# RWKV bonus sums: per-pair columns of ones as weights, tokens streamed in two column tiles

## The reference, cut to what matters

```python
r_h, k_h, v_h, a_h = heads(r), heads(k), heads(v), heads(a)
y = wkv7_scan(r_h, decay, k_h, v_h, -kk, kk * a_h)
mean = jnp.mean(y, -1, keepdims=True)
var = jnp.mean(jnp.square(y - mean), -1, keepdims=True)
y = ((y - mean) * lax.rsqrt(var + GN_EPS)).reshape(B, S, D)
y = y * ln_w.astype(f32) + ln_b.astype(f32)
bonus = jnp.sum(r_h * k_h * r_k.astype(f32), -1, keepdims=True) * v_h
y = (y + bonus.reshape(B, S, D)).astype(h.dtype)
return (y * g) @ w_o
```

## Time and profile before

| | |
|---|---|
| median of 3 runs | 1690.89 us (1688.22 to 1691.16) |
| profiled execution | 1693.16 us, span 1691.3 us |
| PE busy | 1655.3 us (98%) |
| DVE, ACT, POOL busy | 64%, 56%, 67% |
| mean granted clock of TensorE | 0.996 of full speed |

### The profile page before, as it was taken

How to read it: one execution, slowest core, us unless ns; L and a number is a source line. 1 busy time by engine, 2 the same in 40 slices (tenths; PEclk the granted TensorE clock), 3 DMA queues, 4 the chain that set the end, 5 groups by cost and what they waited for, 6 DMA issues and landing times.

```text
span 1691.3 us, 32104 instructions
## 1 busy us (share of the span) xinstructions
PE 1655.3 (98%) x11894; PEld 1459.8 (86%) x11894; DVE 1075.0 (64%) x1978; ACT 948.4 (56%) x1417; POOL 1134.6 (67%) x504
## 2 busy tenths in 40 slices
PE   8999999999999999999999999999999999999998
PEld 6888889999999998887787878888888899888887
DVE  5324242997546666678898985455557975755555
ACT  5458553445544444555555657666567842356555
POOL 6974776788889898786676447665577451746463
PEclk9999999999999999999999999999999999999999
DMA  8544444566655555689999945465553412155552
GB/s 306 200 149 144 155 150 175 163 197 188 189 169 172 155 161 156 195 311 349 357 380 403 411 180 178 182 204 194 191 169 113 168 27 78 53 189 187 196 185 76
DMA packets 96095, 330.10 MB, mean 195 GB/s; under 512 B 32928, under 2 KB 33456, under 8 KB 78592
## 3 DMA queue, kind: packets, MB, share of 16 engines
q1 hardware_dynamic: 84544, 295.06, 51.4%
q0 software_dynamic: 11312, 33.68, 5.3%
q10 hardware_dynamic: 144, 0.07, 0.0%
HBM read 322.47 MB, written 5.24 MB: 194 GB/s over the span
## 4 chain that ended last, share of the span: by engine, by line
PE 59%; POOL 14%; issue 8%; DVE 8%; ACT 7%; DMA 3%; DVEq 0%; ACTq 0%; POOLq 0%; SPq 0%
POOL rows_lo L3115 7%; PE bank L897 7%; PE bank L903 4%; PE bank L1092 4%; PE bank L640 4%; PE bank L1236 4%; PE bank L646 4%; PE bank L641 4%; POOL stat L3146 3%; PE bank L1113 3%; PE bank L929 3%; DMA gathered<-in_v,picked_row 3%; PE bank L972 2%; ACT up_hi L1995 2%; PE bank L1096 2%
## 5 line engine op out<-in xcount | busy, mean ns | idle before, releaser
L3100 POOL TENSOR_TENSOR unit_lo<-unit_raw,unit_hi 128x2048 fp32r<-128x2048 f32 (+1 forms) x86 | 337.3, 3943 | 147.1 <-ACT unit_hi L1715 120.9
L3115 POOL TENSOR_TENSOR rows_lo<-rows_raw,rows_hi 128x1024 fp32r<-128x1024 f32 x128 | 309.4, 2418 | 72.9 <-ACT rows_hi L1835 46.0
L3190 POOL TENSOR_TENSOR up_lo<-up_raw,up_hi 128x2048 fp32r<-128x2048 f32 x22 | 111.2, 5056 | 156.6 <-ACT up_hi L1995 126.8
L1913 ACT ACTIVATE rows_hi<-rows_raw 128x1024 fp32r<-128x1024 f32 x128 | 135.8, 1061 | 124.3 <-PE bank L972 101.4
L2678 DVE TENSOR_TENSOR rows_lo<-rows_raw,rows_hi 128x1024 fp32r<-128x1024 f32 x128 | 159.2, 1249 | 25.3 <-ACT rows_hi L1913 22.0
L1715 ACT ACTIVATE unit_hi<-unit_raw 128x2048 fp32r<-128x2048 f32 x70 | 134.0, 1919 | 65.4 <-PE bank L646 36.8
L1092 PE MATMUL bank<-x_lo_hi,up_hi 128*128 128x512 f32 x640 | 159.8, 392 | 0.0
L903 PE MATMUL bank<-x_lo_hi,rows_lo 128*128 128x256 f32 x1024 | 143.3, 283 | 0.5 <-POOL rows_lo L3115 0.5
L903 PEld LDWEIGHTS bank<-x_lo_hi,rows_lo 128*128 128x128 f32 x1024 | 135.7, 190 | 6.4 <-POOL rows_lo L3115 0.9
L3153 POOL DMA_INDIRECT gathered<-in_v,picked_row x64 | 92.4, 1444 | 69.9 <-DVE bank L2668 57.8
L1092 PEld LDWEIGHTS bank<-x_lo_hi,up_hi 128*128 128x128 f32 x640 | 116.2, 189 | 21.6
(11 more groups left out here) (509 smaller groups left out, 4185.2 us busy)
## 6 DMA issues: line engine op xcount, KB each, us to landing
unit_raw<-in_ring SPq DMA_DIRECT2D x69, 1024.0 KB, 4.9
rows_raw<-in_u SPq DMA_DIRECT2D x128, 512.0 KB
rows_raw<-in_v SPq DMA_DIRECT2D x128, 512.0 KB
up_raw<-in_up SPq DMA_DIRECT2D x44, 1024.0 KB, 5.0
down_raw<-in_down SPq DMA_DIRECT2D x22, 1024.0 KB, 4.9
unit_raw<-in_ring SPq DMA_DIRECT2D x20, 256.0 KB, 3.7
kept_hidden<-table SPq DMA_DIRECT2D x16, 256.0 KB, 4.1
const<-in_const SPq DMA_DIRECT2D x1, 1792.0 KB, 14.2
```

The costliest lines, as they stand in the source:

```text
L1913: A(rows_hi[q % 2][:, :], rows_raw[q][:, :], ACT.Copy).then_inc(S("v_hi_ready"), 1)
L3100: return nc.gpsimd.tensor_tensor(unit_lo[SLOT_OF[n]][:, w], unit_raw[SLOT_OF[n]][:, w], hi, ALU.subtract)
L3115: nc.gpsimd.tensor_tensor(rows_lo[q][:, :], rows_raw[q][:, :], rows_hi_f[q % 2], ALU.subtract).then_inc(S("u_lo_ready"), 1)
```

## The change

The weights become 16 columns of ones and zeros. `two_heads` is a strip of 32 columns with two columns of ones in its middle (one for each half of the partitions), and `pair_of_heads(p)` is a window of 16 columns on it whose ones stand in columns 2p and 2p + 1. The tokens stream: for each pair, 128 columns of `bonusT` for each half of the tokens, into partitions 0 to 15 (th = 0) and 64 to 79 (th = 1) of one bank, `("bh",)`, where the eight pairs add up. ScalarE copies the two 16x128 results to `by_head_bonus`. TensorE goes on with `x_of_chunk(3)` and then turns them to tokens with one product each (16 rows, identity of 16 columns) into the same `("bo", th)` as before, which ScalarE copies on as before. GpSimd fills the strip with three memsets while it sets up the mixer, ahead of the signal `zeroed`.

```diff
+    two_heads = view("two_heads", CONST_AT["iota"][0] + DK, [4 * PAIRS])
+    pair_of_heads = lambda p: two_heads[:, 2 * (PAIRS - p):2 * (PAIRS - p) + 2 * PAIRS]
+    by_head_bonus = view("by_head_bonus", EXTRA_AT + 512, [P])
+    of_heads = lambda th: slice(DK * th, DK * th + 2 * PAIRS)
...
-            def bonus_sums(th):
-                o = fill(("bo", th))
+            def bonus_by_head():
+                o = fill(("bh",), TC)
+                ends = [None] * TC
                 for p in range(PAIRS):
-                    t = mm(o[:, 2 * p:2 * p + 2], bonusT[:, p, th * P:(th + 1) * P], C("head_ones")[:, 0:P:DK], start=True, stop=True)
-                full(("bo", th), t)
+                    for th in range(TC):
+                        ends[th] = mm(o[of_heads(th), 0:P], pair_of_heads(p), bonusT[:, p, th * P:(th + 1) * P], start=p == 0, stop=p == PAIRS - 1, skip_group_check=True)
+                full_by_heads(("bh",), ends)
+
+            def bonus_turned():
+                wait_drained(pe, ("bh",))
+                for th in range(TC):
+                    r = of_heads(th)
+                    o = fill(("bo", th))
+                    full(("bo", th), mm(o[:, 0:2 * PAIRS], by_head_bonus[r, :], ident[r, r], start=True, stop=True))
...
+            pe.wait_ge(S("zeroed"), 1)
             pe.wait_ge(S("bonus_scaled"), 1)
-            for th in range(TC):
-                bonus_sums(th)
+            bonus_by_head()
             c = NRC - 1
             x_of_chunk(c)
+            bonus_turned()
             pe.wait_ge(S("vst_loaded"), 16 * 8)
             step_rhs(0)
...
+            def bonus_by_head():
+                o = wait_filled(act, ("bh",))
+                for th in range(TC):
+                    t = A(by_head_bonus[of_heads(th), :], o[of_heads(th), 0:P], ACT.Copy)
+                drain(("bh",), t)
+
...
+            bonus_by_head()
             for th in range(TC):
                 bonus_sums(th)
...
+            step(nc.gpsimd.memset(two_heads[:, :], 0.0))
+            for par in range(2):
+                step(nc.gpsimd.memset(two_heads[head(par), 2 * PAIRS + par:2 * PAIRS + par + 1], 1.0))
             step(nc.gpsimd.memset(starts[:, :], 1.0))
```

## The result

The median after is 1699.89 us (1695.66 to 1702.18, 6 runs) against 1690.22 us for the kernel before in as many runs beside it: 1.0058 times as long, 95% interval 1.0045 to 1.0071. The profiled execution has a span of 1700.0 us, 8.7 more.

What follows compares the result with a forecast made beforehand. TensorE (PE), busy 98% of the span, was taken as the bound. Wait 10.81 + products 12.59 - 12.75 before = 10.65 us later, less 4.1 gained: 6.55 us slower, 1697.4 us; range 1693.6 to 1702.0, first case's own 1694.5 to 1701.

Steps and rivals of the forecast that it cites:

- the gain: Bonus stretch: 9.61 us become 5.00, 4.61 less; about 0.5 us lost waiting at r2, 4.1 us left.
- the products behind the wait: Output products of the first tokens: 10.89 us plus 1.7 us for a low clock after idling, 12.59 us.
- the wait: First output products: fill on bank 0 waits for the drain of chunk 3's output, 10.81 us later.
- the forecast's first case: Gain of 4.1 us at the bonus, output products wait on bank 0: 1697.4 us, chance 0.71.
- its marks: Fast new sums, full clock through 1425, PE idle about 11 us before the output products, then half clock there.
- rival 2: Bonus stretch: low clock not the old sums' doing, or comes with new ones; gain 2.3 us, 1699.2 us, chance 0.12.
- Rival 4: New bonus sums: the two column tiles don't overlap, 1.87 us more, +8.4 us, 1699.3 us, chance 0.04.
- The shifts: GpSimd's two `rows_shift` behind the bonus delay `first_sum(3)`, so chunk 3's `r2` waits about 0.5 us.
- I let it all move by 4.1 us: Recurrence and chain behind chunk 3's `r2`: all of it moves earlier by the 4.1 us left of the bonus gain.
- the bound of 2.3: Lower bound of the gain left from the bonus stretch, 2.3 us, taken from the low-clock case.
- Rival 5: Output products don't wait, since chunk 3's output is drained in time; only the gain is left, 1686.8 us, chance 0.06.
- Rival 3: Output products: the wait comes, but the clock holds or is back at once; +4.9 us, 1695.7 us, chance 0.07.

Runs made afterwards that it cites:

- the loads spread: Changed kernel with chunk 3's output fixed in bank 7, plus pieces of the first three output-weight units issued after later fills: median 1688.86 us, ratio 0.9982.
- the turn only: Kernel before, with the turn of the banks moved one further ahead of the bonus sums and nothing else: 1700.5 us against 1690.1, ratio 1.0057.
- bank 7: Changed kernel with chunk 3's output put into bank 7 by a fixed number, not the bank of chunk 2's output: 1688.48 us against 1690.1, ratio 0.9991.

## Why the prediction came true, and which terms were off

The forecast was +6.55 us, 1697.4 as a median, own range 1694.5 to 1701; the ratio stands for 9.8 us (7.6 to 12.0), the profile for 8.88. So 1699.89 is inside the range, but 6.55 us is less than the interval allows: three terms were off, the gain by 1.8 us and the products behind the wait by 0.7, both towards slower, and the wait by 0.2 the other way. The mechanism is the forecast's first case, and each of its marks is there. The time alone would have fitted rivals 2 and 4 (1699.2 and 1699.3) better; it is the rows that rule them out.

*The sums and the clock.* 1.87 us forecast, 1.86 measured; the clock stays full from the sums on, so rival 2 is out; the old sums in two pieces kept it full as well, so here it fell with 32 of their records at one go and not with 16. The stretch to chunk 2's turning: 5.00 forecast, 5.06 measured. Rival 4, the rule on row groups of the Trainium skill ("TensorE: Matmul & The Clock Gate", Part 3, The mechanism), is out: 1.86 us in two tiles, though both use all rows, and 3.60 us in one.

*The shifts.* r2 was to wait 0.5 us behind GpSimd. The profile names 0.29 us of it, and with GpSimd's order changed r2 comes 0.49 us earlier. At r2 the gain is 15.04 - 10.98 = 4.06 us; 4.1 was forecast.

*The gain further on: mis-sized.* "I let it all move by 4.1 us" is the step that failed. At the turning of the first tokens 52.91 - 50.60 = 2.31 us are left. The timeline of PE of the kernel before has these rows:

```profile
1436.31 0.68 PE L1236 MATMUL bank<-vst,rk_ak 64*64 64x64 f32 x16 [0.42 <-issue]
...
1439.62 1.15 PE L1236 MATMUL bank<-st,r_k_a 64*64 64x64 f32 x32
...
1446.11 0.74 PE L1236 MATMUL bank<-vst,ktok 64*64 64x64 f32 x18 [1.37 <-issue]
```

Up to the products with `st` and `r_k_a`, whose results DVE and GpSimd go on with, 24.10 us became 21.86 (1437.31 - 1415.45): of 4.06 us gained at r2, 2.24 are left, and nearly all of the loss comes in this part. The kernel before has one stall there, of 0.42 us, the new one two, of 0.83 and 1.22 us, and each costs about 0.2 us more than its idle time, as the run with the loads spread shows, which has none here. From there the chains of GpSimd and DVE move by the same 2.2 us (GpSimd's first low part starts 30.43 us in, where it was 32.66), so the third stall (0.87 us, before 1.37) is no loss of its own: PE then waits 0.31 us for the inverse turned by DVE, which it did not before. The run with the turn only shows that the two trade places: its stall there is 0.28 us, its wait for the inverse 0.90 us, and the first tokens are turned at 52.92 us, as before. So the gain that is kept depends on stalls that differ from run to run. That it came out at the bound of 2.3 is luck: that bound was worked out for a low clock (rival 2), which did not come.

*The bank.* From the turning of the first tokens to the first output product it is 63.88 - 50.60 = 13.28 us, where it was 2.65: 10.63 later, forecast 10.81. Shown from both sides: the number that undoes the shift takes 11.5 us off the stretch, and the shift alone adds 11.45 to the kernel before. Rival 5, no wait, is out.

*The clock behind the wait: mis-sized, 0.7 us.* The output products of the first tokens take 1492.63 - 1479.33 = 13.30 us; 12.59 was forecast. The first three groups took 1484.34 - 1479.33 = 5.01 us where 2.72 are three groups at full clock: 2.3 us lost, not the 1.7 that the wait in the expert part showed. Rival 3, no loss, is out.

Sum: +10.63 at the wait, +0.55 in the products, -2.31 gained is +8.87, as in the profile.

*What the stalls wait for.* No run here changes when instructions come, but the DMA view of the traces points at TensorE's own instructions. The page of the kernel after lists a DMA queue that moves instructions in packets of 16 KB (packets, MB, share):

```profile
q8 instruction: 64, 1.05, 0.3%
```

and one such packet is seen in the window 1430 to 1432.6, ahead of the second stall:

```profile
q8 instruction: 1, 0.02, 2.5%
```

In windows of 0.1 us, the packets ahead of the three stalls begin at 1426.25, 1431.45 and 1440.75; the stalls end at 1428.76, 1433.87 and 1443.18, 2.4 to 2.5 us later. Over the twelve profiles, each of the 28 stalls ends 2.2 to 2.7 us after such a packet began. Their places fit too: from the first stall of the kernel after to the second are 127 records, from the second to the third 254, and in the kernel before 253 from one to the other. Where a packet came early enough there is no stall: one begins at 1434.95, and TensorE is 127 records behind the second stall only at about 1437.6. So it looks as if the stalls stand where a new block of instructions begins, and last until it is there. What stays open is why a packet comes when it does, and so why a stall varies between 0 and 1.95 us.

## What to carry to other kernels

Where buffers are handed out in turn while the program is built, one more buffer moves all that follow it, and a fixed number further on can fall on one that is still in use: list the buffers and their last readers again after every added fill, far behind the edit too. Here a run of 32 records that streamed two columns each let the clock fall although TensorE was not idle; cutting the run in two with other products between gave 3.0 of the 4.55 us that the rewrite of the products gave at this place, though the time of that run shows no gain (1.0003). A gain in the middle of a tightly coupled stage is worth what TensorE's own stalls and the other engines' chains behind it leave, so look for the next wait before counting it at the end. And where a stretch ends at an idle time, read the clock behind it before comparing two edits by some tenths of a microsecond.

## What the runs showed of the hardware that was not expected

A VectorE operation on 128x8 elements (the scaling of the row variance) took 0.17 us before, 0.62 us after and 1.18 us with bank 7, at the same place beside GpSimd's low parts of the output weights. The timelines of DVE and POOL of the run with bank 7:

```profile
1442.74 1.18 DVE L2946 TENSOR_SCALAR stat<-stat 128x8 f32<-128x8 f32 x1
```

```profile
1441.39 5.40 POOL L3121 TENSOR_TENSOR unit_lo<-unit_raw,unit_hi 128x512 fp32r<-128x512 f32 x4
```

of the kernel after:

```profile
1447.78 0.62 DVE L2946 TENSOR_SCALAR stat<-stat 128x8 f32<-128x8 f32 x1
```

```profile
1445.88 5.40 POOL L3121 TENSOR_TENSOR unit_lo<-unit_raw,unit_hi 128x512 fp32r<-128x512 f32 x4
```

and of the kernel before, where a window cuts off GpSimd's later pieces and so shows the length of two:

```profile
1450.60 0.17 DVE L2925 TENSOR_SCALAR stat<-stat 128x8 f32<-128x8 f32 x1
```

```profile
1448.18 2.51 POOL L3100 TENSOR_TENSOR unit_lo<-unit_raw,unit_hi 128x512 fp32r<-128x512 f32 x2
```

It starts 1.35, 1.90 and 2.42 us after GpSimd's first piece, and ends 2.53, 2.52 and 2.59 us after it: two pieces take 2.51 us. So it lasts until GpSimd's running piece ends, and its length is only a matter of when it starts. The run with the turn only, with the old sums, agrees: started 1.32 us after the first piece it took 1.21 us. The Trainium skill ("SBUF — State Buffer", Who interferes with whom) states that a `tensor_scalar` can enter a mode in which VectorE and GpSimd contend for a shared pair of ports, and that whoever issues first has the pair for the whole instruction while the other waits; these rows agree, though none shows the mode. It fits that the turn that stood behind this operation on DVE came late, and that putting the turn first gave 0.8 us of the stretch.
